# GpSimd's scaling of the first head in the second mixer's attention: a product with a repeated column in place of a tensor-scalar instruction

## Chip, cores and metric

The kernel runs on one core of one Trainium2 chip, in one launch. The metric is the time of an execution on the device in microseconds (us). Before the change the median of three runs is 1896.23 us; the three are 1896.23, 1896.23 and 1899.35 us.

## What is computed

Two blocks in sequence over 512 tokens of width 1024, all in float32: an mLSTM mixer and a sparse-attention mixer (the "second mixer" here, `nsa_mixer`), and then a block of RWKV-7 beside differential attention, with a feed-forward part and a gated projection. The change lies in the attention of the second mixer. Its core, cut to what matters:

```python
p = masked_softmax(jnp.einsum('bqghd,bgqkd->bghqk', qb, kg) * scale, mask)      # selected blocks
o_sel = jnp.einsum('bghqk,bgqkd->bqghd', p.astype(vg.dtype), vg)
...
p = masked_softmax(jnp.einsum('bqghd,bkgd->bghqk', qb, kb) * scale, mask)       # window
o_win = jnp.einsum('bghqk,bkgd->bqghd', p.astype(vb.dtype), vb)
...
gate = jax.nn.sigmoid(g_logit + b_gate)
o = gate[..., 0:1] * heads(o_cmp) + gate[..., 1:2] * heads(o_sel) + gate[..., 2:3] * heads(o_win)
return (o.reshape(B, S, NSA_INNER) * jax.nn.silu(z)) @ w_out
```

There are 16 heads of 64 columns in 4 groups. With 512 tokens all blocks are selected and the window spans everything, so both branches are causal softmax attention, each with keys and values of its own. Each row of a head's probabilities is multiplied by its gate over its sum; that product is the weight of the row.

## The kernel before, in words

The program is one list of stages. Each stage gives every engine (TensorE, ScalarE, VectorE, GpSimd, and SyncE for DMAs) a list of its own, run in order; the engines meet only at semaphores. The order of the work is written out by hand, and there is no planner.

`stage_nsa_attention` (line 1781) works on 64 units. A unit is a pair of heads, 128 query rows and a branch (selected or window). `units` orders them: for each of four pairs of head tiles, query blocks 3, 2, 1, 0, and in each of these four units (two branches by two tiles). Block i has keys of `length` (i+1) x 128, so the columns per head of four units in a row are 512, then 384, 256 and 128; then it starts over with 512. There are 16 units of each length.

What happens in unit m, by engine:

- TensorE computes the scores of both heads into two PSUM banks (mask products at L1864, score products at L1873).
- VectorE takes the negated row maximum (L1977).
- ScalarE computes the exponential of each head into `att_p` in SBUF, with the row sums (L1936, head 0 and head 1 in turn).
- VectorE takes the reciprocal of both sums (L1995), and multiplies by the gates (L2000, 128x2), which gives the weight columns `sm(32, m)`; this increments `w_done`.
- The two heads are then scaled in place by their weight columns: GpSimd takes head 0 (L1836, the line of the change) and increments `scaled0`; VectorE takes head 1 (L2003) and increments `scaled1`. Both wait for `w_done` only.
- TensorE waits for `scaled0`, `scaled1` and for the copies of the unit before, and transposes both heads into PSUM (L1892: 16, 12, 8 or 4 transposes, each in two halves by partitions, recorded as that many loads and products).
- The transposes are copied to `att_pt`: ScalarE alone at 512 columns (L1947), else ScalarE (L1951) and VectorE (L2012) a half each.
- After every second unit TensorE multiplies by the values (L1906 and L1913), and VectorE writes the output times z to `att_y` (L1989) after every fourth.

TensorE's list is: scores of unit n+1, transposes of unit n-2, and in every second step the value products of units n-4 and n-3. `att_p` has three buffers. The weight columns have four, so L2000 of unit m also waits for `scaled0` and `scaled1` of unit m-4, long done.

GpSimd's list of the stage holds L1836 for the 64 units, and behind eight of them (units 8 to 15) four casts and four differences of the second half's queries (`high`, L1826, and `low`, L1830). The lines of the loop before the change:

```python
            for m in range(U):
                L = length(m)
                pool.wait_ge(s["w_done"], m + 1)
                pool.tensor_scalar(p[:, m % 3, 0, 0:L], p[:, m % 3, 0, 0:L], sm(32, m)[:, 0:1], None, ALU.mult) \
                    .then_inc(s["scaled0"], 1)
```

In front of this stage stands `stage_nsa_in`, and behind it `stage_add` with the output projection (L300, L301, L305). Elsewhere GpSimd runs some products and differences of two tensors that the prediction uses as rows: L685 (`widen`, 128 columns, both inputs repeated columns: one in groups of four), L1830, L2405 (512 columns, one input a column repeated over groups of 64), L2969 (512 columns in place, times columns repeated over groups of 128), and one tensor-scalar instruction with two operations, L2415 (512 columns).

Of the kernel before, what the change touches and what calls it, by code (L numbers as in the profile page):

```python
# [8 lines left out]
ALU = mybir.AluOpType  # L9
# [3 lines left out]
P = 128  # L13
# [1767 lines left out]
def stage_nsa_attention(k):  # L1781
# [3 lines left out]
    p = k.region("att_p", [P, 3, 2, S], F32, 16)  # L1785
# [3 lines left out]
    s = {n: k.sem(f"att_{n}") for n in (  # L1789
          "sc_mm", "nm_done", "exp_done", "tr_mm", "pt0", "pt1", "pv_mm", "y_done",  # L1790
          "step", "w_done", "scaled0", "scaled1", "y_hi", "y_lo", "q_hi", "q_lo")}
# [7 lines left out]
    def length(n):  # L1799
        return (units[n][1] + 1) * P  # L1800

    def sm(base, n):
        return k.small[:, base + 2 * (n % 4):base + 2 * (n % 4) + 2]

    def copied(eng, m):

        eng.wait_ge(s["pt1"], m + 1)
        own = sum(i < TT - 1 for _, i, _ in units[:m + 1])
        if own:
            eng.wait_ge(s["pt0"], own)  # L1810
# [6 lines left out]
    def query_high(t):  # L1817
        if t < 4:
            return k.q_hi[t // 2][:, t % 2, :]
        return (k.act_hi, k.act_lo)[t // 2 % 2][:, 5 + 2 * (t % 2), :]  # L1820

    with k.joined() as block:
        @block.gpsimd
        def _(pool):
            def high(t):
                pool.tensor_copy(query_high(t), k.q[:, t, :]).then_inc(s["q_hi"], 1)  # L1826

            def low(t):
                pool.wait_ge(s["q_hi"], t - 3)
                pool.tensor_tensor(k.q_lo[:, t, :], k.q[:, t, :], query_high(t).bitcast(F32), ALU.subtract) \  # L1830
                    .then_inc(s["q_lo"], 1)

            for m in range(U):
                L = length(m)
                pool.wait_ge(s["w_done"], m + 1)
                pool.tensor_scalar(p[:, m % 3, 0, 0:L], p[:, m % 3, 0, 0:L], sm(32, m)[:, 0:1], None, ALU.mult) \  # L1836
                    .then_inc(s["scaled0"], 1)
                if 8 <= m < 16:
                    (high, low)[m % 2](m // 2)

# [1960 lines left out]
```

## Time and profile before

| what | value |
|---|---|
| median of three runs | 1896.23 us |
| the three runs | 1896.23, 1896.23, 1899.35 us |
| the profiled execution's own time | 1899.72 us |
| its span, first to last instruction | 1898.0 us |
| mean granted TensorE clock in it | 0.987 of full |
| the stage of the change | about 628 to 775 us of the span |
| L1836, 64 instructions | 81.8 us busy on GpSimd |

The profile is of one execution, which lay 3.49 us above the median. Its parts are busy time per engine, the slices of the span, DMA queues, the chain of waits that ended last, groups of instructions by line, and DMA issues. In a row of a group: engine, operation, output and inputs by the program's names, shapes, count, then busy us in total and mean ns of one, then the engine's idle time just before them with what ended it. In the timeline: start us, duration us, engine, line, operation, and in brackets the idle time before with its releaser. PE is TensorE's multiplying, PEld its weight loading, DVE VectorE, ACT ScalarE, POOL GpSimd. PEclk is the granted clock, 1.00 being 2.4 GHz and 0.50 being 1.2 GHz.

### The profile page before, as it was taken

The page shows a single profiled execution, that of the slowest core. Times are in us where ns is not written, and L with a number is a line of the kernel's source. Part 1 is how long each engine was busy: PE and PEld are TensorE (multiplying, and loading weights), DVE is VectorE, ACT ScalarE, POOL GpSimd, SP SyncE. Part 2 cuts the span into 40 slices and gives each one's busy share as a digit, 9 for nine tenths or more (in the row PEclk, how much of TensorE's full clock was granted, in tenths as well). Part 3 has the DMA queues.
Part 4 walks back from the last instruction along what each step waited for, and adds up shares of the span by engine and source line. Part 5 has one row for each costly group of instructions (what it writes and reads, how often), then busy time and mean ns, then how long its engine had stood idle before and what let it go on. Part 6 is the DMA issues. An engine that isn't in the chain of part 4 may idle for free. (4 is left out here: it accounts for less than half of the span.)

```text
span 1898.0 us, 36850 instructions
## 1 busy us (share of the span) xinstructions
PE 1824.1 (96%) x15870; PEld 1484.7 (78%) x15870; DVE 1095.2 (58%) x1644; ACT 675.3 (36%) x1100; POOL 308.9 (16%) x292
## 2 busy tenths in 40 slices
PE   8999999999999788999999899999999999999997
PEld 6877757688888567778888669888878888888886
DVE  4664354553257788444366887778574635354545
ACT  4334332332223577442222374433233322122342
POOL 4210011130002565320021240000001000000011
PEclk9999999999999899999999999999999999999998
DMA  5334323142223010134421100002042322322221
GB/s 191 103 111 134 136 83 133 45 190 101 90 74 111 35 37 12 49 109 138 137 102 56 48 2 4 4 3 70 4 178 92 104 104 89 111 89 89 78 100 45
DMA packets 42848, 160.87 MB, mean 85 GB/s; under 512 B 5312, under 2 KB 14528, under 8 KB 28096
## 3 DMA queue, kind: packets, MB, share of 16 engines
q1 hardware_dynamic: 28480, 143.84, 22.1%
q10 hardware_dynamic: 14208, 14.68, 2.2%
q8 instruction: 126, 2.06, 0.4%
q14 instruction: 34, 0.28, 0.0%
HBM read 140.42 MB, written 16.78 MB: 83 GB/s over the span
## 5 line engine op out<-in xcount | busy, mean ns | idle before, releaser
L257 DVE TENSOR_TENSOR wlo<-raw,whi 128x2048 fp32r<-128x2048 f32 (+2 forms) x113 | 251.0, 2221 | 179.2 <-ACT whi L248 178.8
L248 ACT ACTIVATE whi<-raw 128x2048 fp32r<-128x2048 f32 (+2 forms) x113 | 209.0, 1850 | 320.8 <-PE ps L283 161.4
L281 PE MATMUL ps<-act_hi,whi 128*128 128x512 f32 x616 | 243.1, 395 | 0.0
L301 PE MATMUL ps<-act_lo,whi 128*128 128x512 f32 x632 | 242.7, 393 | 0.0
L283 PE MATMUL ps<-act_hi,wlo 128*128 128x512 f32 x616 | 240.6, 391 | 0.0
L282 PE MATMUL ps<-act_lo,whi 128*128 128x512 f32 x616 | 240.5, 390 | 0.0
L300 PE MATMUL ps<-act_hi,whi 128*128 128x512 f32 x592 | 236.4, 399 | 0.0
L305 PE MATMUL ps<-act_hi,wlo 128*128 128x512 f32 x632 | 156.5, 389 | 0.0
L301 PEld LDWEIGHTS ps<-act_lo,whi 128*128 128x128 f32 x632 | 120.2, 190 | 25.9 <-issue 1.2
L305 PEld LDWEIGHTS ps<-act_hi,wlo 128*128 128x128 f32 x632 | 118.6, 188 | 24.7
L300 PEld LDWEIGHTS ps<-act_hi,whi 128*128 128x128 f32 x592 | 111.6, 188 | 32.5 <-issue 8.2
L283 PEld LDWEIGHTS ps<-act_hi,wlo 128*128 128x128 f32 x616 | 116.0, 188 | 24.5
L281 PEld LDWEIGHTS ps<-act_hi,whi 128*128 128x128 f32 x616 | 116.1, 189 | 24.3 <-issue 0.5
L282 PEld LDWEIGHTS ps<-act_lo,whi 128*128 128x128 f32 x616 | 116.0, 188 | 24.0 <-issue 0.5
L3439 PE MATMUL ps<-f_lo,whi 128*128 128x512 f32 x256 | 99.6, 389 | 0.0
L3440 PE MATMUL ps<-f_hi,wlo 128*128 128x512 f32 x256 | 99.6, 389 | 0.0
L3438 PE MATMUL ps<-f_hi,whi 128*128 128x512 f32 x256 | 99.6, 389 | 0.0
L1836 POOL TENSOR_SCALAR att_p<-att_p,small 128x512 f32<-128x512 f32 (+3 forms) x64 | 81.8, 1279 | 70.7 <-DVE small L2000 69.6
L1936 ACT ACTIVATE att_p<-ps,small 128x512 f32<-128x512 f32 (+3 forms) x128 | 66.5, 528 | 29.4 <-DVE small L1977 29.0
L3472 DVE TENSOR_TENSOR xT<-xT,ps 128x512 f32<-128x512 f32 x32 | 21.9, 686 | 82.6 <-PE ps L3440 82.6
L3407 ACT ACTIVATE f_hi<-ff_sq 128x512 fp32r<-128x512 f32 x32 | 20.2, 633 | 123.1 <-DVE ff_sq L3463 123.1
L355 POOL TENSOR_TENSOR norm_ple_total<-norm_ple_total,norm_ple_sq 128x512 f32<-128x512 f32 x6 | 7.8, 1296 | 332.0 <-ACT norm_ple_sq L341 332.0
(550 smaller groups left out, 3474.7 us busy)
## 6 DMA issues: line engine op xcount, KB each, us to landing
raw<-stream_in SPq DMA_DIRECT2D x107, 1024.0 KB, 4.9
v_scratch<-v_out ACTq DMA_DIRECT2D x16, 256.0 KB, 3.5
z_scratch<-zt ACTq DMA_DIRECT2D x16, 256.0 KB, 2.9
mlh_v<-v_scratch SPq DMA_DIRECT2D x4, 1024.0 KB, 4.8
mlh_z<-z_scratch SPq DMA_DIRECT2D x16, 256.0 KB, 2.6
cmp_w<-cmp_w_in SPq DMA_DIRECT2D x2, 2048.0 KB, 11.3
z_scratch<-in_zt ACTq DMA_DIRECT2D x16, 256.0 KB, 3.2
mix_g<-z_scratch SPq DMA_DIRECT2D x16, 256.0 KB, 6.6
```

The costliest lines, as they stand in the source:

```text
L248: act.activation(k.whi[b % 2][:, 0:n], k.raw[b % RAW_SLOTS][:, 0:n], ACT.Copy).then_inc(k.hi_done, 1)
L257: dve.tensor_tensor(k.wlo[b % 2][:, 0:n], k.raw[b % RAW_SLOTS][:, 0:n], k.whi[b % 2][:, 0:n].bitcast(F32), ALU.subtract).then_inc(k.lo_don ...
L281: pe.matmul(bank, hi, x_hi, start=(x == 0), stop=False)
L282: pe.matmul(bank, hi, x_lo, start=False, stop=False)
L283: last = pe.matmul(bank, lo, x_hi, start=False, stop=(x == end))
L300: pe.matmul(bank, hi, x_hi, start=(x == 0), stop=False)
L301: pe.matmul(bank, hi, x_lo, start=False, stop=False)
L305: last = pe.matmul(bank, lo, x_hi, start=False, stop=(x == end))
L1836: pool.tensor_scalar(p[:, m % 3, 0, 0:L], p[:, m % 3, 0, 0:L], sm(32, m)[:, 0:1], None, ALU.mult) \
L3438: pe.matmul(k.ps[:, t % 4, :], whi, f_hi[:, kt, :], start=(kt == 0), stop=False)
L3439: pe.matmul(k.ps[:, t % 4, :], whi, f_lo[:, kt, :], start=False, stop=False)
L3440: last = pe.matmul(k.ps[:, t % 4, :], wlo, f_hi[:, kt, :], start=False, stop=(kt == KD - 1))
```

## The change

The product of head 0 with its weight column is written as a product of two tensors, the second being the column repeated over the L columns (stride zero), on the same engine, in place, with the same wait and the same semaphore. Nothing else is touched.

```diff
             for m in range(U):
                 L = length(m)
                 pool.wait_ge(s["w_done"], m + 1)
-                pool.tensor_scalar(p[:, m % 3, 0, 0:L], p[:, m % 3, 0, 0:L], sm(32, m)[:, 0:1], None, ALU.mult) \
-                    .then_inc(s["scaled0"], 1)
+                x = p[:, m % 3, 0, 0:L]
+                pool.tensor_tensor(x, x, sm(32, m)[:, 0:1].to_broadcast([P, L]), ALU.mult).then_inc(s["scaled0"], 1)
                 if 8 <= m < 16:
                     (high, low)[m % 2](m // 2)
```

## Rows read from the trace of the kernel before

**Rows 1.** The profile's page, busy time of each engine, us and share of the span.

```profile
PE 1824.1 (96%) x15870; PEld 1484.7 (78%) x15870; DVE 1095.2 (58%) x1644; ACT 675.3 (36%) x1100; POOL 308.9 (16%) x292
```

**Rows 2.** Busy time in the changed stage: us, PE, PEld, DVE, ACT, POOL, PEclk, DMA.

```profile
628.00:775.00 147.00, 122.64 (x2036) 102.15 (x2034) 118.61 (x325) 103.54 (x326) 89.06 (x72) 0.96 0.06 22
```

**Rows 3.** Groups by line and shape, POOL, the instruction that the change replaces.

```profile
L1836 POOL TENSOR_SCALAR att_p<-att_p,small 128x512 f32<-128x512 f32 x16 | 29.9, 1873 | 24.6 <-DVE small L2000 24.3
L1836 POOL TENSOR_SCALAR att_p<-att_p,small 128x384 f32<-128x384 f32 x16 | 23.5, 1466 | 19.7 <-DVE small L2000 19.6
...
L1836 POOL TENSOR_SCALAR att_p<-att_p,small 128x256 f32<-128x256 f32 x16 | 17.3, 1082 | 13.5 <-DVE small L2000 13.3
...
L1836 POOL TENSOR_SCALAR att_p<-att_p,small 128x128 f32<-128x128 f32 x16 | 11.1, 696 | 12.8 <-DVE small L2000 12.4
```

**Rows 4.** Who waited for whom in the stage: us in total, times, longest.

```profile
PEld ps L1864 <- ACT att_p L1936: 17.2, 28, 1.9
...
PEld ps L1892 <- POOL att_p L1836: 11.4, 17, 1.5
...
PE ps L1892 <- POOL att_p L1836: 6.2, 9, 1.3
```

**Rows 5.** Groups by line and shape, DVE, in the stage.

```profile
L2000 DVE TENSOR_TENSOR small<-small,nsa_gtok 128x2 f32<-128x2 f32 x64 | 13.1, 204 | 2.2
...
L2003 DVE TENSOR_SCALAR att_p<-att_p,small 128x512 f32<-128x512 f32 x16 | 7.9, 493 | 0.6
L2003 DVE TENSOR_SCALAR att_p<-att_p,small 128x384 f32<-128x384 f32 x16 | 6.7, 420 | 0.6
...
L2003 DVE TENSOR_SCALAR att_p<-att_p,small 128x256 f32<-128x256 f32 x16 | 5.7, 353 | 0.6
L2003 DVE TENSOR_SCALAR att_p<-att_p,small 128x128 f32<-128x128 f32 x16 | 4.6, 287 | 0.6
```

**Rows 6.** Timeline, two units of 512 columns in a row.

```profile
743.99 0.49 DVE L2003 TENSOR_SCALAR att_p<-att_p,small 128x512 f32<-128x512 f32 x1
744.05 4.94 POOL L1836 TENSOR_SCALAR att_p<-att_p,small 128x512 f32<-128x512 f32 x3 [1.17 <-DVE small L2000]
...
745.45 0.16 DVE L2000 TENSOR_TENSOR small<-small,nsa_gtok 128x2 f32<-128x2 f32 x1
745.65 0.53 DVE L2003 TENSOR_SCALAR att_p<-att_p,small 128x512 f32<-128x512 f32 x1
...
745.88 1.72 POOL L1836 TENSOR_SCALAR att_p<-att_p,small 128x512 f32<-128x512 f32 x1
```

**Rows 7.** Groups by line and shape, POOL, other stages: products, and a tensor-scalar instruction.

```profile
L685 POOL TENSOR_TENSOR wide_v<-hw,consts 128x128 f32<-128x128 f32 x16 | 7.9, 498 | 82.9 <-PE ps L811 82.9
...
L2969 POOL TENSOR_TENSOR da_o<-da_o,small 128x512 f32<-128x512 f32 x4 | 4.6, 1176 | 0.1
...
L2405 POOL TENSOR_TENSOR rw_first_E<-rw_first_X 128x512 f32<-128x512 f32 x2 | 2.0, 1038 | 0.0
L2415 POOL TENSOR_SCALAR rw_rate<-rw_rate,cols,small 128x512 f32<-128x512 f32 x2 | 2.0, 1015 | 0.0
```

**Rows 8.** Timeline, transposes that GpSimd releases, and a copy in front of one.

```profile
647.64 0.49 ACT L1951 ACTIVATE att_pt<-ps 128x384 f32<-128x384 f32 x1 [0.21 <-PE ps L1892]
...
648.95 0.45 PEld L1892 LDWEIGHTS ps<-consts,att_p 64*128 64x128 f32 x12 [0.99 <-POOL att_p L1836]
...
669.93 0.58 PEld L1892 LDWEIGHTS ps<-consts,att_p 64*128 64x128 f32 x16 [0.26 <-POOL att_p L1836]
...
765.97 0.32 PEld L1892 LDWEIGHTS ps<-consts,att_p 64*128 64x128 f32 x8 [0.24 <-POOL att_p L1836]
...
772.43 0.20 PEld L1892 LDWEIGHTS ps<-consts,att_p 64*128 64x128 f32 x4 [1.45 <-POOL att_p L1836]
```

**Rows 9.** Timeline, VectorE's small product beside a GpSimd difference of two tensors.

```profile
655.04 1.27 POOL L1830 TENSOR_TENSOR nsa_q_lo<-nsa_q,act_hi 128x512 fp32r<-128x512 f32 x1
...
655.72 0.60 DVE L2000 TENSOR_TENSOR small<-small,nsa_gtok 128x2 f32<-128x2 f32 x1
```

## The prediction

> **What bounds the kernel now.** Read the page's busy times first: TensorE is busy for 96% of the span, GpSimd for 16% [rows 1]. GpSimd can only matter where TensorE waits for it, so the next view is the busy time of the changed stage. In its 147 us TensorE is busy 122.6, VectorE 118.6, ScalarE 103.5 and GpSimd 89.1, of which the changed instruction has 81.8 (29.9 + 23.5 + 17.3 + 11.1) [rows 2, 3]. No engine is full; the stage is a ring of four engines in which each is late in turn. The view of waits puts 11.4 us (17 times) and 6.2 us (9 times) of TensorE's idle time in front of the transposes down to L1836, beside 17.2 us in front of the scores to ScalarE's exponential [rows 4]. The 17.6 us are a ceiling that is too high: at 512 columns the transposes mostly begin behind ScalarE's copy of the unit before. In the timeline only 14 of the 64 groups of transposes begin 0.05 us behind L1836's end: four units of 384 columns, four of 256, three of 128 and three of 512. Those are the places where a change of L1836 is seen at once [rows 8].
>
> **The instruction that goes.** L1836 takes 1.87, 1.47, 1.08 and 0.70 us at 512, 384, 256 and 128 columns [rows 3]. Part of that is not its own. It starts 0.06 us behind VectorE's scaling of the other head, released by the same semaphore [rows 6]; where it started late (745.88 us, with 0.30 us left of VectorE's 0.53 us) it took 1.72 us instead of 1.87 [rows 6]. So GpSimd stands still while VectorE's L2003 runs (0.49, 0.42, 0.35 and 0.29 us [rows 5]). Less what is left of that after 0.06 us, its own work is 1.44, 1.11, 0.79 and 0.47 us: 2.5 ns a column.
>
> **The instruction that comes.** The nearest rows are products of two tensors in which one is a repeated column: L2405 takes 1.04 us at 512 columns, and L2969, the same product in place by a repeated column, 1.18 us as a mean beside VectorE's work [rows 7]. I take 1.04, since the share of VectorE's scaling is counted apart. The other end at 512 is L1830's 1.27 us, with both inputs read in full [rows 9]. At 128 columns L685 takes 0.50 us [rows 7] and a quarter of L2405 would be 0.26 us; I take 0.45, nearer to the row of that length, and on the line between it and 1.04 get 0.84 at 384 and 0.65 at 256. So a unit's scaling gets shorter by 0.40, 0.27, 0.14 and 0.02 us. Busy time falls by 16 x 0.83 = 13 us, to some 68.5, and 16 instructions of 512 columns should read 1.47 us instead of 1.87.
>
> **What of it reaches the path.** The four units of 384 columns wait up to 0.99 us in the row shown; behind GpSimd, ScalarE's copy of the unit before is next, 0.82 us earlier (647.64 + 0.49 = 648.13 against 648.95) [rows 8], so the whole 0.27 counts: 4 x 0.27 = 1.1 us. Those of 256 wait at least 0.24 us [rows 8]: 4 x 0.14 = 0.6. Of the three of 512 one waits 0.26 us [rows 8], where TensorE's own scores are next, the other two under 0.15, which I take as 0.1 each: 0.45. Those of 128: 3 x 0.02 = 0.06. Sum 2.2 us. The other 50 units are covered: at 512 columns by ScalarE's copy or TensorE's own list, so that the largest saving, 0.40 us, is mostly spent on waits that someone else ends. Of the 2.2 us some is taken back by the next wait: TensorE comes earlier to the scores, whose 17.2 us of waits hang on ScalarE and VectorE [rows 4], and these move up only where they had waited for the transposes. I keep three quarters, 1.7 us. If the whole came through it would be 2.2; if GpSimd took no time at all, about 4.8 (the 14 waits up to each next releaser, added up in the same timeline).
>
> One term goes the other way. VectorE's small product L2000, with both inputs in SBUF, took 0.16 us at 745.45 us in the middle of an L1836 [rows 6], but 0.60 us at 655.72 us behind GpSimd's difference of two tensors, ending with it [rows 9]; its mean is 0.204 us for that reason [rows 5]. The Trainium skill, "SBUF — State Buffer", section "Who interferes with whom", says that a VectorE instruction with two SBUF inputs and a GpSimd instruction that reads SBUF shut each other out, for the whole of whichever came first. The trace agrees for L1830 and not for L1836. So the new product will hold off L2000 where the next unit's comes before its end. At 512 columns that end is 0.06 + 0.43 + 1.04 = 1.53 us after L2003 starts, and the next L2000 comes 1.46 us after it in the closest pair (743.99 to 745.45) [rows 6]: 0.07 us. I count three such places, 0.2 us together. With 1.27 us instead of 1.04 it would be 0.3 us in such a pair, still under 1 us in all. Nothing is queued on GpSimd that others wait for, except the eight casts and differences of units 8 to 15, which move up with it.
>
> Sum: -1.7 + 0.2 = -1.5 us. The profiled execution (1899.72 us) would become 1898.2, and the median of the runs, 3.49 us below it, 1896.23 - 1.5 = 1894.7 us. About 0.2% (3.8 us) is what a measurement of this kernel can tell from no change; the forecast lies inside it.
>
> **Rivals.**
>
> *The gain is nil* (0.10). The product takes 1.27 us at 512 columns, as for two inputs read in full, and in proportion at the others, or ScalarE's chain takes all of it back. Then 1896.0 us. For it: 17.2 us of TensorE's waits are ScalarE's [rows 4]. Against it: L2405 [rows 7]. The case that the instruction emitted is the old one belongs here; the operation's name in the trace would show it.
>
> *The tensor-scalar form is the quick one* (0.06). L2415, with two operations on 512 columns, took 1.02 us as a mean, part of it beside VectorE's work [rows 7], against 1.44 for L1836. If the missing 0.42 us belongs to the place and not to the form, the product takes 1.04 + 0.42 + 0.43 = 1.89 us and nothing is gained; if the tensor-scalar form alone would take 0.6 us, it takes 1.04 + 0.84 + 0.43 = 2.3, and 14 waits grow by some 0.2 us and a few covered ones come up: 1896.2 + 3 = 1899 us. Against it: L1830, in the same place, took 1.27 us [rows 9]. The Trainium skill, "GPSIMD Engine Reference", section "Engine selection", calls instructions with one input roughly line-rate and those with two inputs about twice as slow as on VectorE; by that the change is a loss. L1836's 1.44 us does not agree.
>
> *The product gets in ahead of VectorE's scaling* (0.05; slower). Today VectorE starts L2003 0.06 us ahead and GpSimd waits [rows 6]. If the product gets there first, L2003 waits for all of it, as L2000 did behind L1830 [rows 9]: 16 x (1.04 + 0.84 + 0.65 + 0.45) = 48 us more on VectorE. It has 147 - 118.6 = 28 us to spare [rows 2], so some 20 us come out: 1916 us. It decides once it happens in more than about half of the units.
>
> *More comes back* (0.09). The granted clock of the stage is 0.96 of full [rows 2], so about 8% of it, 12 us, ran at 1.2 GHz, behind stretches in which TensorE was partly idle. If a fall is avoided through shorter waits, some 3 us more come back: 1891.5 us. A moved fall could also cost as much; that goes into the range.
>
> **Numbers.** The forecast has 0.70, the rivals the rest. The range: below, 1896.2 less the ceiling of 4.8, 1891.4; above, the second rival with the spread of the runs shown (3.1 us over the median in one of three), 1899.4. Out of it lie the third rival and tails. Faster by over 0.2% is the fourth rival and a tail of the forecast: 0.12. Slower by over 0.2% is the third and part of the second: 0.09. Within: 0.79.
>
> **What would show it.** L1836 as TENSOR_TENSOR of 1.47, 1.20, 0.94 and 0.68 us; the waits of L1892 for GpSimd down from 17.6 us by several us, with ScalarE's copy named in their place; L2003 unchanged at 0.49 us; L2000's mean at 0.21 us; the stage 1 to 2 us shorter. L2003 at over 1 us would be the third rival; L1836 over 1.87 us the second. The forecast is wrong if the stage moves by more than 5 us either way.

## The result, and the profile after

The changed kernel takes 1913.76 us (median of 4, 1912.42 to 1915.83) against 1897.79 us for the kernel before in the same comparison (4 runs, 1896.23 to 1900.68). The ratio is 1.0079 with an interval of 1.0063 to 1.0094: slower by 16 us by the medians (12 to 18 by the interval), where 1.5 us less was forecast. It is the third rival that came true, priced at 1916 us and given a chance of 0.05. The profiled execution took 1915.83 us, its span 1914.1 us.

In the two profiled executions all of it lies in the changed stage. The last product by the values, beside which the output projection begins, as the timeline of TensorE shows it, before and then after:

```profile
774.54 1.08 PE L1913 MATMUL ps<-att_pt,nsa_vtok 128*64 128x128 f32 x8 [0.48 <-DVE att_pt L2012]
```

```profile
790.68 1.12 PE L1913 MATMUL ps<-att_pt,nsa_vtok 128*64 128x128 f32 x8 [0.48 <-DVE att_pt L2012]
```

It starts 16.1 us later, and the span is longer by 1914.1 - 1898.0 = 16.1 us. The groups by line and shape of the changed kernel's stage (count, then busy us and mean ns) answer to [rows 3, 5]; the changed instruction is now L1837:

```profile
L2003 DVE TENSOR_SCALAR att_p<-att_p,small 128x512 f32<-128x512 f32 x16 | 21.9, 1367 | 0.6
...
L2003 DVE TENSOR_SCALAR att_p<-att_p,small 128x384 f32<-128x384 f32 x16 | 17.4, 1086 | 0.6
...
L1837 POOL TENSOR_TENSOR att_p<-att_p,small 128x512 f32<-128x512 f32 x16 | 16.6, 1040 | 43.5 <-DVE small L2000 43.5
...
L1837 POOL TENSOR_TENSOR att_p<-att_p,small 128x384 f32<-128x384 f32 x16 | 13.2, 827 | 32.6 <-DVE small L2000 32.6
...
L2003 DVE TENSOR_SCALAR att_p<-att_p,small 128x256 f32<-128x256 f32 x16 | 12.9, 806 | 0.6
...
L2000 DVE TENSOR_TENSOR small<-small,nsa_gtok 128x2 f32<-128x2 f32 x64 | 10.6, 165 | 2.2
L1837 POOL TENSOR_TENSOR att_p<-att_p,small 128x256 f32<-128x256 f32 x16 | 9.8, 613 | 24.8 <-DVE small L2000 24.8
...
L2003 DVE TENSOR_SCALAR att_p<-att_p,small 128x128 f32<-128x128 f32 x16 | 8.4, 526 | 0.6
...
L1837 POOL TENSOR_TENSOR att_p<-att_p,small 128x128 f32<-128x128 f32 x16 | 6.4, 400 | 20.2 <-DVE small L2000 20.0
```

Two things are to be seen. GpSimd's instruction takes 1.04, 0.83, 0.61 and 0.40 us, and none of it is waiting (without any overlap, in run 1 below, it takes the same); the own work was forecast as 1.04, 0.84, 0.65 and 0.45. And L2003, which nobody touched, went from 0.49, 0.42, 0.35 and 0.29 us [rows 5] to 1.37, 1.09, 0.81 and 0.53. That is 60.6 us in place of 24.9, 35.7 more on VectorE. The timeline of one unit, where both instructions follow the same semaphore:

```profile
633.96 1.37 DVE L2003 TENSOR_SCALAR att_p<-att_p,small 128x512 f32<-128x512 f32 x1
634.00 1.04 POOL L1837 TENSOR_TENSOR att_p<-att_p,small 128x512 f32<-128x512 f32 x1 [1.76 <-DVE small L2000]
```

VectorE still has the earlier start stamp, but GpSimd goes through and VectorE ends 0.29 us after it. VectorE's next row maxima are late by that, and the views of waits of the stage show where it goes. Before:

```profile
ACT att_p L1936 <- DVE small L1977: 29.0, 43, 1.9
...
PE ps L1864 <- ACT att_p L1936: 11.4, 17, 1.2
```

In the changed kernel:

```profile
ACT att_p L1936 <- DVE small L1977: 47.2, 59, 2.3
PEld ps L1864 <- ACT att_p L1936: 29.7, 29, 1.9
PE ps L1864 <- ACT att_p L1936: 23.8, 26, 1.7
...
PEld ps L1892 <- POOL att_p L1837: 4.5, 4, 1.4
```

ScalarE's wait for the row maxima grew from 29.0 to 47.2 us. TensorE's waits for the exponentials grew from 17.2 [rows 4] to 29.7 us for the weight loads and from 11.4 to 23.8 us for the products; the two are not to be added up, since loads and products wait side by side. The loads' wait of the transposes for GpSimd did fall, from 11.4 us [rows 4] to 4.5 us. So the gain that the change was to bring is there, and the waits behind VectorE outweigh it.

The clock has a part in the time too. The changed kernel's stage ran at a lower mean granted clock than the stage before, 0.92 in place of 0.96 [rows 2]:

```profile
628.00:791.00 163.00, 129.93 (x2034) 109.09 (x2032) 148.49 (x325) 104.45 (x326) 53.48 (x72) 0.92 0.06 20
```

From 776.8 us to the stage's end it was granted 0.50, which is 1.2 GHz. In the 26.8 us before that, from 750 us, TensorE was busy for 21.3 us. A second profile of the same kernel, run 10's, has it busy for 21.4 us there, nearly the same waits (47.8, 29.8 and 23.5 us) and the same L2003. But in it no stretch at 1.2 GHz behind 750 us lasted over 3.4 us, its stage ran at 0.97, and the last product by the values starts at 784.36 us in place of 790.68. So of the 16 us of this profile some 6 go with the clock, as far as two profiles show it, and about 10 are there at a clock no lower than before. Over whole executions the granted clock was 0.984 to 0.987 here and 0.982 to 0.987 in run 10, against 0.986 to 0.989 in the seven executions of the kernel before beside run 10. Whether the longer waits bring the lower clock about was not tested.

### The profile page after: what moved, and what is told of

It is laid out like the page before. It is cut to its first block and busy times, and to the rows that moved or that the text cites. A ratio compares the mean times of both kernels' runs of the same rounds, so it can differ in the third digit from the quotient of the medians.

```text
span 1914.1 us, 36850 instructions
## 1 busy us (share of the span) xinstructions
PE 1830.5 (96%) x15870; PEld 1491.0 (78%) x15870; DVE 1125.1 (59%) x1644; ACT 676.5 (35%) x1100; POOL 273.7 (14%) x292
## 5 line engine op out<-in xcount | busy, mean ns | idle before, releaser
L1936 ACT ACTIVATE att_p<-ps,small 128x512 f32<-128x512 f32 (+3 forms) x128 | 66.4, 524 | 47.2 <-DVE small L1977 47.2
L1837 POOL TENSOR_TENSOR att_p<-att_p,small 128x512 f32<-128x512 f32 (+3 forms) x64 | 46.1, 720 | 121.1 <-DVE small L2000 120.9
L2003 DVE TENSOR_SCALAR att_p<-att_p,small 128x512 f32<-128x512 f32 (+3 forms) x64 | 60.6, 946 | 2.3
```

The lines of the kernel that those rows point to most:

```text
L1936: act.activation(p[:, n % 3, e, 0:L], k.ps[:, 2 * (n % 2) + e, 0:L], ACT.Exp, bias=sm(0, n)[:, e:e + 1], accum_out=sm(8, n)[:, e:e + 1]).t ...
```

## Experiments

**Theory A.** The two scalings shut each other out, whoever comes first goes through, and in the changed kernel that is GpSimd. VectorE's list (the instructions it has to run in order) grows by 35.7 us, and that is the 16 us. Head 0 is GpSimd's, head 1 VectorE's. **Rivals**: the product costs something else on the path; the form of the instruction decides and not the order; any two instructions on this buffer disturb each other; the loss is that head 1 is ready late. Each time given for before is from runs on the same chip as the experiment's.

**1. No overlap.** GpSimd's product waits for VectorE's scaling to be done.

```diff
-                pool.wait_ge(s["w_done"], m + 1)
+                pool.wait_ge(s["scaled1"], m + 1)
                 x = p[:, m % 3, 0, 0:L]
                 pool.tensor_tensor(x, x, sm(32, m)[:, 0:1].to_broadcast([P, L]), ALU.mult).then_inc(s["scaled0"], 1)
```

> GpSimd's product waits for scaled1 (VectorE's L2003 done) instead of w_done, so the two never overlap. Theory A (the two shut each other out for the whole instruction, and in the changed kernel the product got in first, which alone cost the 16 us): L2003 back to 0.49, 0.42, 0.35, 0.29 us, the product unchanged at 1.04, 0.83, 0.61, 0.4 us, head 0 ready about 1.6 us behind L2003's start at 512 columns against 1.93 before; the kernel 1 to 2 us below the kernel before (ratio 0.999), 16 us below the changed one. Rival B (the product costs something else on the path, such as a late completion or ScalarE being slowed): L2003 short again, but the kernel stays more than 5 us above the kernel before.

Measured: 1900.07 us against 1900.77, ratio 0.9997 (0.9988 to 1.0006). L2003 is back at 0.49 us, and the product takes 1.04 us in 15 of the 16 units of 512 columns (1.42 in one, in which it comes upon another instruction of VectorE's, L1968):

```profile
L1837 POOL TENSOR_TENSOR att_p<-att_p,small 128x512 f32<-128x512 f32 x16 | 17.0, 1064 | 35.5 <-DVE att_p L2003 35.5
...
L2003 DVE TENSOR_SCALAR att_p<-att_p,small 128x512 f32<-128x512 f32 x16 | 7.8, 487 | 0.6
```

The whole loss is gone with the overlap, so rival B of this run falls. Whether the expected gain of 1 to 2 us came cannot be told: the interval holds it and holds no change.

**2. The instruction of before, without overlap.** The same edit on the tensor-scalar form.

```diff
-                pool.wait_ge(s["w_done"], m + 1)
+                pool.wait_ge(s["scaled1"], m + 1)
                 pool.tensor_scalar(p[:, m % 3, 0, 0:L], p[:, m % 3, 0, 0:L], sm(32, m)[:, 0:1], None, ALU.mult) \
```

> The kernel before with its tensor-scalar instruction waiting for scaled1 in place of w_done. Theory (1.87 us at 512 columns was 1.44 of its own behind 0.43 of waiting for L2003): it takes 1.44, 1.11, 0.79, 0.47 us and ends 0.06 us later than before relative to L2003's start; the kernel within 0 to 3 us of before. Rival (the length is all its own, or comes from the place and not from L2003): it still takes 1.87, 1.47, 1.08, 0.70 us, and the kernel is 6 us or more slower than before.

```profile
L1836 POOL TENSOR_SCALAR att_p<-att_p,small 128x512 f32<-128x512 f32 x16 | 26.0, 1623 | 29.1 <-DVE att_p L2003 29.1
...
L1836 POOL TENSOR_SCALAR att_p<-att_p,small 128x384 f32<-128x384 f32 x16 | 19.9, 1246 | 22.5 <-DVE att_p L2003 22.5
...
L2003 DVE TENSOR_SCALAR att_p<-att_p,small 128x512 f32<-128x512 f32 x16 | 8.4, 526 | 0.6
```

1905.55 us against 1900.77, ratio 1.0023 (1.0013 to 1.0034), between the two expectations. The tensor-scalar instruction takes 1.57 us at 512 columns in most units (1.62 as a mean) and 1.25 at 384. So its wait for VectorE before was 0.30 us of 1.87, not the 0.43 that I took off; its own work is 1.57, not 1.44.

The same trace shows VectorE waiting for the tensor-scalar instruction. In four units L2003 came while L1836 of the unit before was still well under way. With 0.49 us of L1836 left, L2003 took 0.77 us at 512 columns in place of 0.49; with 0.44 and 0.43 us left it took 0.65 at 384 in place of 0.42. Each time it is longer by what was left of L1836, less 0.20 us.

**3. A pad of one small instruction.** GpSimd gets a memset of one spare column between the wait and the product, which moves the product's start from 0.044 to 0.081 us behind L2003's (the trace's own nanoseconds; the timeline rounds to 0.01 us).

```diff
                 pool.wait_ge(s["w_done"], m + 1)
+                pool.memset(k.small[:, 60 + m % 8:61 + m % 8], 0.0)
                 x = p[:, m % 3, 0, 0:L]
```

> The changed kernel with one memset of a single spare column on GpSimd between the wait for w_done and the product, which puts the product some 0.1 us later and takes nothing else away. Theory A (who comes first decides): VectorE's L2003 now gets in first and takes 0.49 us at 512 columns, the product waits and takes about 1.04 + 0.35 = 1.4 us; the kernel within 2 us of before. Rival B (the form decides, a product of two tensors holds VectorE's scaling off whichever came first, or both are slowed by sharing): L2003 stays at 1.2 us or more and the kernel 14 to 20 us above the kernel before.

```profile
L1838 POOL TENSOR_TENSOR att_p<-att_p,small 128x512 f32<-128x512 f32 x16 | 20.8, 1302 | 0.0
...
L2004 DVE TENSOR_SCALAR att_p<-att_p,small 128x512 f32<-128x512 f32 x16 | 7.8, 486 | 0.6
...
L1836 POOL MEMSET small<- 128x1 f32 x64 | 6.3, 98 | 89.9 <-DVE small L2001 89.6
```

Now VectorE goes through at 0.49 us (here L2004), and the product waits: 1.30 us, its own 1.04 and 0.26 behind VectorE. These are the same two instructions, released by the same semaphore, and 0.037 us decide. The kernel takes 1897.88 us against 1900.77, ratio 0.9984 (0.9975 to 0.9994): it is faster than both the kernel before and the changed one, by 1.1 to 4.8 us against before. The order decides for the product, and rival B of this run falls.

**4. The other order, a little.** The kernel before, with an extra reciprocal on VectorE in front of L2003.

```diff
                     dve.wait_ge(s["w_done"], m + 1)
                     L = length(m)
+                    dve.reciprocal(k.small[:, 60:62], sm(24, m))
```

> The kernel before with a second reciprocal of two columns (0.155 us, result unused) on VectorE between w_done and L2003, so that GpSimd's tensor-scalar instruction is the first of the two by about 0.1 us. Theory A (order alone decides, for every form): L2003 now waits for all of it and takes 1.3 us or more at 512 columns, the tensor-scalar instruction 1.44 us. Rival B (GpSimd's tensor-scalar form never holds VectorE off and yields whenever VectorE comes): L2003 stays at 0.49 us and the tensor-scalar instruction at 1.87 us.

One execution, 1900.16 us. The numbers are rival B's, but the run did not test what it was meant to: the reciprocal overlapped with the scaling and moved it by 0.08 us only, so that GpSimd had a lead of 0.02 us where 0.1 was meant. L2003 (here L2004) took 0.47 us and the tensor-scalar instruction 1.84. It shows that the tensor-scalar form loses the race even with a lead of 0.02 us, where the product wins from 0.04 us behind.

**5. The other order, clearly.** Three reciprocals, into columns of their own.

```diff
                     dve.wait_ge(s["w_done"], m + 1)
                     L = length(m)
+                    for i in range(3):
+                        dve.reciprocal(k.small[:, 44 + 2 * (3 * (m % 8) + i):46 + 2 * (3 * (m % 8) + i)], sm(24, m))
```

> The kernel before with three extra reciprocals of two columns on VectorE between w_done and L2003 (results unused), so that GpSimd's tensor-scalar instruction starts about 0.3 us ahead of L2003 instead of 0.06 us behind it. Theory A (first come holds the other off, for the tensor-scalar form as well; it only gets going later than the product does): the tensor-scalar instruction takes 1.57 us or a little less at 512 columns and L2003 takes 1.4 us or more. Rival B (the form decides; the tensor-scalar form always gives way to VectorE): L2003 0.49 us, the tensor-scalar instruction 1.85 us.

One execution, 1904.84 us against a median of 1899.84. The timeline of GpSimd and then VectorE in one unit; the lead is 0.14 us where 0.3 was expected:

```profile
669.28 1.56 POOL L1836 TENSOR_SCALAR att_p<-att_p,small 128x512 f32<-128x512 f32 x1 [0.29 <-DVE small L2000]
```

```profile
669.22 0.29 DVE L2004 RECIPROCAL small<-small 128x2 f32<-128x2 f32 x3
669.42 0.82 DVE L2005 TENSOR_SCALAR att_p<-att_p,small 128x512 f32<-128x512 f32 x1
```

Neither theory is right. VectorE's scaling takes 0.82 us, 0.33 more than alone, and ends at 670.24 us, 0.60 us before the tensor-scalar instruction does at 670.84, which was not lengthened at all (1.56 us). So with this lead GpSimd's tensor-scalar form slows VectorE down but does not hold it to its end, as the product does. The delay is not a fixed time either: it is 0.33, 0.23, 0.12 and 0.01 us at 512, 384, 256 and 128 columns. In run 2, where the same form was 1.1 us under way, VectorE did wait to its end. What makes the difference was not found out.

**6. VectorE's form.** The changed kernel, with L2003 also writing out the sum of its row.

```diff
-                    dve.tensor_scalar(p[:, m % 3, 1, 0:L], p[:, m % 3, 1, 0:L], sm(32, m)[:, 1:2], None, ALU.mult) \
-                        .then_inc(s["scaled1"], 1)
+                    dve.tensor_scalar(p[:, m % 3, 1, 0:L], p[:, m % 3, 1, 0:L], sm(32, m)[:, 1:2], None, ALU.mult,
+                                      ALU.add, accum_out=k.small[:, 60 + m % 8:61 + m % 8]).then_inc(s["scaled1"], 1)
```

> The changed kernel (product on w_done, no pad) with VectorE's L2003 also writing out the sum of its row to a spare column, an instruction form that runs at one element a cycle. Theory A (only VectorE's fast form of this instruction needs what GpSimd also needs): both run side by side, the product 1.04 us, L2003 about 0.6 to 0.7 us at 512 columns plus a short second instruction for the sum; the kernel 2 to 8 us above before, 8 to 14 below the changed one. Rival C (any two instructions on the same buffer disturb each other): L2003 stays at 1.3 us or more.

```profile
L1837 POOL TENSOR_TENSOR att_p<-att_p,small 128x512 f32<-128x512 f32 x16 | 16.7, 1042 | 36.7 <-DVE small L2000 36.7
...
L2003 DVE TENSOR_SCALAR_CACHE_REDUCE att_p<-att_p,small 128x512 f32<-128x512 f32 x16 | 11.9, 746 | 0.6
```

The two run side by side on the same buffer, 1.04 and 0.75 us. Rival C, a disturbance by the buffer, falls. The kernel takes 1898.23 us against 1899.84, ratio 0.9991 (0.9981 to 1.0001), where 2 to 8 us above before were expected: the slower form of VectorE's instruction, 0.26 us longer at 512 columns, makes the kernel some 15 us faster than the quick one does beside the product. VectorE's list is 15.4 us longer than before all the same, 10.1 in L2003 and 5.3 in a read-out of 0.08 us behind each, so the loss is not in proportion to what VectorE's list gains. The Trainium skill, "SBUF — State Buffer", section "Who interferes with whom", says that VectorE's tensor-scalar instructions in their two-port mode and GpSimd's shut each other out for the whole instruction, and excepts the form that writes out its accumulator. Runs 3 and 6 agree, and so does the changed kernel, in which L2003 goes on to 0.28 us behind the product's end. For GpSimd's tensor-scalar form run 2 agrees and run 5 does not.

**7. Part of the change.** The product at 512 columns only.

```diff
-                pool.tensor_tensor(x, x, sm(32, m)[:, 0:1].to_broadcast([P, L]), ALU.mult).then_inc(s["scaled0"], 1)
+                if L == 512:
+                    pool.tensor_tensor(x, x, sm(32, m)[:, 0:1].to_broadcast([P, L]), ALU.mult).then_inc(s["scaled0"], 1)
+                else:
+                    pool.tensor_scalar(x, x, sm(32, m)[:, 0:1], None, ALU.mult).then_inc(s["scaled0"], 1)
```

> The product only in the 16 units of 512 columns, the tensor-scalar instruction in the other 48. Theory A with VectorE as the price: L2003 1.37 us in those 16 units and as before in the rest, 14.0 of the 35.7 us that VectorE gained in the changed kernel, so about 14.0 / 35.7 x 16 = 6.3 us above before (4 to 9). Rival D (at 512 columns ScalarE's copies and TensorE cover VectorE's delay, and the loss comes from the short units): under 3 us above before.

1904.62 us against 1899.84, ratio 1.0026 (1.0015 to 1.0037), 4.8 us, with 12.2 us more on VectorE. That is as theory A has it; rival D is all but excluded (the interval begins just under its 3 us). The trace holds a comparison that was not planned. In 14 of the 16 units the product starts 43 or 44 ns behind L2003 (here L2006) and wins; in two, the first of the third and of the fourth pair of tiles, it starts 49 ns behind and loses. The first of these two and the unit after it, GpSimd and then VectorE (the printed starts, rounded, hide the 6 ns):

```profile
705.30 1.33 POOL L1838 TENSOR_TENSOR att_p<-att_p,small 128x512 f32<-128x512 f32 x1 [1.21 <-DVE small L2003]
707.53 1.04 POOL L1838 TENSOR_TENSOR att_p<-att_p,small 128x512 f32<-128x512 f32 x1 [0.89 <-DVE small L2003]
```

```profile
705.25 0.49 DVE L2006 TENSOR_SCALAR att_p<-att_p,small 128x512 f32<-128x512 f32 x1
...
707.48 1.37 DVE L2006 TENSOR_SCALAR att_p<-att_p,small 128x512 f32<-128x512 f32 x1
```

**8. The price of VectorE's list.** The version with the pad, and behind L2003 a filler of about the length that L2003 had gained.

```diff
                         .then_inc(s["scaled1"], 1)
+                    dve.tensor_reduce(k.small[:, 68 + m % 8:69 + m % 8],
+                                      k.consts[:, 0:{512: 740, 384: 540, 256: 345, 128: 140}[L]], AX, ALU.max)
```

> The version with the pad (L2003 at 0.49 us) with a filler on VectorE behind L2003 of the length that L2003 had gained in the changed kernel: a maximum over 740, 540, 345 or 140 columns of constants, about 0.87, 0.66, 0.45 and 0.24 us, into a spare column. Theory A (the 16 us are VectorE's longer list and nothing else): 14 to 19 us above the kernel before. Rival E (part of the loss is that head 1 is ready late, so that TensorE's transposes wait): under 10 us above before, since here head 1 is ready as early as before.

1910.65 us against 1899.84, ratio 1.0061 (1.0044 to 1.0078): 11.6 us above before (8.4 to 14.8), between the expectations. So the longer list alone costs most of what the changed kernel loses. The filler put 38.8 us on VectorE. Against run 3's ratio, across two comparisons, it is 0.0077, or 14.6 us, for VectorE's list alone, while head 1 was ready early; the changed kernel stands 0.0086 to 0.0095 above run 3, or 16 to 18 us. In the two profiled executions with the same mean clock of 0.987, this one and run 10's, the last product by the values starts at 784.35 and 784.36 us.

**9. The filler in front.** The same with the filler between the wait for `w_done` and L2003, so that head 1 is late too.

```diff
                     dve.wait_ge(s["w_done"], m + 1)
                     L = length(m)
+                    dve.tensor_reduce(k.small[:, 68 + m % 8:69 + m % 8],
+                                      k.consts[:, 0:{512: 740, 384: 540, 256: 345, 128: 140}[L]], AX, ALU.max)
```

> As the version with pad and filler (11.6 us above before), but the filler on VectorE stands in front of L2003, so that head 1 is late by the filler too and GpSimd's product is over or nearly so when L2003 comes. If the missing part of the changed kernel's loss is that head 1 is ready late, this one lies at 14 to 18 us above before, within 3 us of the changed kernel; if it lies at 10 to 13 us, the missing part is something else.

1917.53 us against 1901.16, ratio 1.0085 (1.0067 to 1.0104), 16 us, as expected if head 1's lateness counts. But L2003 took 0.56 us in place of 0.49, as the product was not quite over, so VectorE's list had some 43 us more, against 35.7 in the changed kernel.

**10. The changed kernel again**, beside run 9.

> The changed kernel itself, on the same chip as the filler in front, for that comparison: 14 to 18 us above before; L2003 at 1.37 us in all 16 units of 512 columns, the product 0.043 to 0.046 us behind it in each.

1913.03 us against 1901.16, ratio 1.0070 (1.0045 to 1.0094): 13 us (9 to 18), where 14 to 18 were expected. L2003 took 1.37 us in all 16 units of 512 columns, with the product 0.043 to 0.046 us behind its start in every unit. Runs 8 to 10 have intervals that overlap. VectorE's longer list accounts for most of the loss; how much the lateness of head 1 adds, and how much of the time comes by way of the clock, stays open.

## Why the prediction was wrong

*The instruction that goes.* Off in size: its own work is 1.57 us (run 2), not 1.44. L2003's share in 1.87 us was 0.30, not 0.43: at every length L1836 was longer before than alone by L2003's time less 0.20 us (1.87 against 1.57 at 512 columns, 0.70 against 0.61 at 128), so the first 0.20 us of L2003 held up nobody.

*The instruction that comes.* Right: 1.04 us at 512 columns, from L2405's row; a little under the forecast at the short lengths (0.61 and 0.40 against 0.65 and 0.45).

*"So GpSimd stands still while VectorE's L2003 runs."* This is the step that failed. It was true of the instruction of before, and I carried it over to the new one: "At 512 columns that end is 0.06 + 0.43 + 1.04 = 1.53 us after L2003 starts". The rows gave the order of two start stamps 0.06 us apart [rows 6], and I took the order of the stamps for the order in which the data are claimed. The new form starts 0.044 us behind in place of 0.058, and in all 64 units L2003 waited for it: 1.37 us in place of 0.49 at 512 columns, 35.7 us in all.

An estimate from the rows shows how close the race is. L2003 is delayed by what is left of the other instruction less 0.20 us: 0.88 us with 1.08 left behind the product, 0.28 with 0.49 left in run 2, 0.05 with 0.25 left in the kernel before. So its claim comes about 0.20 us after its start stamp. Once L2003 is through, the product needs 0.90 of its 1.04 us (run 3), so its claim comes about 0.14 us after its stamp. By that a product that starts up to some 0.06 us behind is still the first to claim; run 7 puts the turn between 0.044 and 0.049 us. The tensor-scalar form does not fit this picture: it lost even from 0.02 us ahead (run 4), so the form matters beside the stamp.

The rows held two warnings. Behind a GpSimd difference VectorE waits to its end [rows 9], which I used only for L2000. And L2003 took 0.53 us in place of 0.49 where L1836 had 0.25 us left [rows 6], which by the estimate above is a wait to L1836's end: whoever was well under way held off the other in this very pair. The third rival named the mechanism and deserved far more than 0.05.

*What of it reaches the path.* Not refuted where the premise holds. With the order of before restored (run 3), the kernel is 1.1 to 4.8 us faster than before; the sum said 1.5, from a saving of 0.40 us a unit at 512 columns where run 3's was 0.53 (1.38 in place of 1.91 us behind L2003's start). The loads' wait of the transposes for GpSimd fell there from 11.4 to 4.6 us. The 0.2 us that the sum charged for L2000 cannot be seen: the product ends sooner than thought in run 3 (0.081 + 1.302 = 1.38 us behind L2003's start, not 1.53), and L2000's mean fell, from 0.204 us to 0.180 in run 3 and 0.165 in the changed kernel.

*The third rival's price.* Its 48 us on VectorE were 35.7, because L2003's first part passes beside the product: it adds 0.88 us, not 1.04. The 28 us of spare time of VectorE did not absorb as much as the subtraction took off (16 of the 36 came out, where the subtraction leaves 8), probably since its idle time sits in places that the ring of waits makes; no run shows this by itself. The two errors pull in opposite ways, so that 20 us priced and 16 measured lie close together by luck in part; and the price left out the clock, which has a share in the 16.

*The first two rivals and the fourth.* The product did not take 1.27 us, and the tensor-scalar form is slower in itself (1.57 against 1.04), so what the Trainium skill, "GPSIMD Engine Reference", section "Engine selection", states, that instructions with one input are roughly line-rate and those with two the slow ones, does not hold for this form here. The fourth rival, a gain by the clock, did not come; in the profile after the clock moved the other way, by more than the some 3 us that the prediction allowed a moved fall to cost.

## What to carry to other kernels

When two engines are released by one semaphore and contend, a change of one instruction's form can reverse which goes first, and the engine that pays is then the other one, whose code nobody touched. Start stamps do not tell who claims first: ask what happens if the order flips, and give that case real weight. If the order matters, make it explicit. A tiny instruction in front of the one that should yield (here a memset of 0.1 us) turned a loss of 13 to 16 us into a gain of about 3; and the slower form of VectorE's instruction, which does not contend, was nearly as good.

## What was not expected of the hardware

- A few nanoseconds of head start decide: at 42 to 46 ns for VectorE's scaling (all 64 units of the changed kernel) GpSimd's product wins, and VectorE takes 1.37 us at 512 columns; at 49 ns VectorE takes 0.49 us and the product 1.33. In one kernel both occurred (run 7).
- GpSimd's tensor-scalar form at 128x512 takes 1.57 us alone (run 2), its product with a repeated column 1.04; per further column 2.5 ns ((1.56 - 0.60) / 384, both from run 5, where it was not delayed) against 1.67 ns ((1.04 - 0.40) / 384).
- GpSimd's tensor-scalar form has two ways with VectorE's scaling. When it is first by 0.14 us, VectorE's takes 0.82 us in place of 0.49 and ends 0.60 us before it (run 5). When it is under way for 1.1 us, VectorE's waits to its end (0.77 us with 0.49 left, run 2). The product lets nothing through in either case.
